# First ordinary tile of three feed-forward blocks in two other PSUM banks, norm factor spread one item earlier, eight weight loads issued behind a barrier

## The reference

```
def swiglu(x, w_gate, w_up, w_down):
    return (jax.nn.silu(x @ w_gate) * (x @ w_up)) @ w_down

for layer in range(2):
    h = h + 0.5 * swiglu(rms_norm(h, norm_ffn[layer, 0]), ...)     # ffn2 (layer 0), ffn4 (layer 1)
    hn = rms_norm(h, norm_mix[layer])
    h = h + (pool_fox_mixer(hn, ...) if layer == 0 else mla_mixer(hn, ...))
    h = h + 0.5 * swiglu(rms_norm(h, norm_ffn[layer, 1]), ...)     # ffn3 (layer 0), ffn5 (layer 1)
```

## Time and profile before

| | before |
| --- | --- |
| three runs, us | 2809.74, 2806.75, 2810.09 (median 2809.74) |
| profiled execution: its own time | 2809.01 us |
| its span, first to last instruction | 2807.1 us |
| PE busy | 2697.0 us (96% of the span) |
| DVE busy | 1757.4 us (63%) |
| ACT busy | 1122.8 us (40%) |
| mean granted TensorE clock | 0.982 |

### The profile page before, as it was taken

How to read it: one execution, slowest core, us unless ns; L and a number is a source line. 1 busy time by engine, 2 the same in 40 slices (tenths; PEclk the granted TensorE clock), 3 DMA queues, 4 the chain that set the end, 5 groups by cost and what they waited for, 6 DMA issues and landing times. The chain is left out here.

```text
span 2807.1 us, 46580 instructions
## 1 busy us (share of the span) xinstructions
PE 2697.0 (96%) x18452; PEld 2263.1 (81%) x18452; DVE 1757.4 (63%) x3031; ACT 1122.8 (40%) x2077; POOL 358.6 (13%) x261
## 2 busy tenths in 40 slices
PE   7989898999999999999999999999999989999998
PEld 5868755778888788888868999989999845889997
DVE  3454668453232643335457888888888656688885
ACT  3232235522211421213265444454444446654444
POOL 2000123421112230212301000010000100100000
PEclk9999989999999999999999999999999999999999
DMA  8250310123332233323303333333332340323331
GB/s 274 62 166 23 103 38 5 61 85 96 96 100 82 83 105 93 102 81 111 88 7 85 99 102 102 95 102 98 91 113 83 75 109 1 90 76 106 98 106 53
DMA packets 346456, 248.75 MB, mean 89 GB/s; under 512 B 28148, under 2 KB 341304, under 8 KB 346240
## 3 DMA queue, kind: packets, MB, share of 16 engines
q1 hardware_dynamic: 346034, 245.71, 29.3%
q10 hardware_dynamic: 206, 0.06, 0.0%
HBM read 241.52 MB, written 2.12 MB: 87 GB/s over the span
## 5 line engine op out<-in xcount | busy, mean ns | idle before, releaser
L2972 ACT CAST dense_wt_hi<-ring 128x512 fp32r<-128x512 f32 x554 | 343.1, 621 | 350.0 <-PE bank L3023 177.5
L2977 DVE TENSOR_TENSOR dense_wt_lo<-ring,dense_wt_hi 128x512 fp32r<-128x512 f32 x554 | 381.6, 691 | 99.8 <-ACT dense_wt_hi L2972 98.9
L3010 PE MATMUL bank<-dense_operand_hi,dense_wt_hi 128*128 128x256 f32 x960 | 272.9, 284 | 7.5 <-DVE h L3500 6.7
L3012 PE MATMUL bank<-dense_operand_hi,dense_wt_lo 128*128 128x256 f32 x960 | 272.3, 284 | 0.0
L3011 PE MATMUL bank<-dense_operand_lo,dense_wt_hi 128*128 128x256 f32 x960 | 272.2, 284 | 0.0
L575 DVE TENSOR_TENSOR dense_wt_lo<-ring,dense_wt_hi 128x2048 fp32r<-128x2048 f32 (+1 forms) x67 | 166.3, 2482 | 155.2 <-ACT dense_wt_hi L560 155.2
L560 ACT CAST dense_wt_hi<-ring 128x2048 fp32r<-128x2048 f32 (+1 forms) x67 | 124.4, 1857 | 306.7 <-PE bank L802 301.1
L3023 PE MATMUL bank<-dense_act_hi,dense_wt_hi 128*128 128x512 f32 x656 | 203.8, 392 | 1.0 <-DVE dense_act_lo L3289 1.0
L3023 PE MATMUL bank<-dense_act_lo,dense_wt_hi 128*128 128x512 f32 x656 | 202.8, 390 | 0.0
L3023 PE MATMUL bank<-dense_act_hi,dense_wt_lo 128*128 128x512 f32 x656 | 202.3, 390 | 0.0
L802 PE MATMUL bank<-feat_lo,dense_wt_hi 128*128 128x512 f32 x640 | 197.1, 389 | 0.0
(11 more groups left out here) (702 smaller groups left out, 5900.7 us busy)
## 6 DMA issues: line engine op xcount, KB each, us to landing
ring<-in_ffn_w_up SPq DMA_DIRECT2D x66, 512.0 KB, 3.8
ring<-in_ffn_w_gate SPq DMA_DIRECT2D x66, 512.0 KB, 5.1
ring<-in_ada_w SPq DMA_DIRECT2D x24, 1024.0 KB, 7.5
ring<-in_ffn_w_down SPq DMA_DIRECT2D x40, 512.0 KB, 4.8
ring<-in_ffn_w_down SPq DMA_DIRECT2D x48, 256.0 KB, 3.8
ring<-in_w_ffn_gate SPq DMA_DIRECT2D x11, 1024.0 KB, 5.4
ring<-in_w_ffn_up SPq DMA_DIRECT2D x11, 1024.0 KB, 5.4
ring<-in_ffn_w_gate SPq DMA_DIRECT2D x11, 1024.0 KB, 5.3
```

Of the source, the lines that this page charges most:

```text
L2972: self.nc.scalar.copy(self.wh[:, i % BLOCKS, :], src).then_inc(self.s_high, 1)
L2977: self.nc.vector.tensor_tensor(self.wl[:, i % BLOCKS, :], self.items[i][1], self.wh[:, i % BLOCKS, :].bitcast(F32), ALU.subtract).then_inc ...
L3010: pe.matmul(out, h[:, w], xh, start=start and k == 0, stop=False, skip_group_check=shared)
L3012: last = pe.matmul(out, l[:, w], xh, start=False, stop=stop and k == 3, skip_group_check=shared)
```

## The change

Tile 0 of each of the three blocks goes to banks 4 and 5; tile 1 stays in 2 and 3. The column sums and the spread factor move from banks 4 and 5 to 6 and 7. P1 and P5 of tile 2 no longer wait for tile 0's product. Items 0 and 1 get a wait for the previous part's additions out of banks 4 and 5. The spread is issued ahead of item 5 instead of item 6. The eight loads at the end of the MLA preparation are issued by SP in the attention stage, behind the barrier.

```
         for b in range(TB):
-            last = pe.matmul(K.bank[4][:, b:b + 1], K.h[:, 0, b * P:(b + 1) * P], K.k("ones")[:, 0:1], start=True, stop=True)
+            last = pe.matmul(K.bank[6][:, b:b + 1], K.h[:, 0, b * P:(b + 1) * P], K.k("ones")[:, 0:1], start=True, stop=True)
...
-            last = pe.matmul(K.bank[5][:, b * P:(b + 1) * P], self.col[:, b:b + 1].broadcast_to([P, P]), K.k("ident"), start=True, stop=True)
+            last = pe.matmul(K.bank[7][:, b * P:(b + 1) * P], self.col[:, b:b + 1].broadcast_to([P, P]), K.k("ident"), start=True, stop=True)
...
-    wide = lambda u, m: K.bank[2 * (u % 2) + m][:, :]
+    wide = lambda u, m: K.bank[(4, 2)[u] + m][:, :]
...
+            if n in (0, 1):
+                pe.wait_ge(prev.done[0], prev.done[1] - 2)
+
...
-            if p in ("P1", "P5") and u < PLAIN + 2:
+            if p in ("P1", "P5") and u == PLAIN + 1:
                 pe.wait_ge(s_act, u - 1)
+            elif u == PLAIN and p in ("P1", "P5"):
+                pass
...
-            if n == 6:
+            if n == 5:
                 now.spread(pe)
...
                         sp.dma_start(B.Q[64:96, 4 * g + j, :], K.h[32 * j:32 * j + 32, g, :]).then_inc(s_moved, 16)
-                K.stream(sp, plan.end("mla_v") + RING)
                 sp.wait_ge(s_moved, 16 * 18)
...
-                        bias=lambda h, i: B.mask[:, 384 - i * P:384 - i * P + (i + 1) * P])
+                        bias=lambda h, i: B.mask[:, 384 - i * P:384 - i * P + (i + 1) * P],
+                    loads=lambda sp: K.stream(sp, K.plan.end("mla_v") + RING))
```

More of the change, by code:

```diff
@@ L3222, in root @@
         act.wait_ge(self.s_sum, 1)
-        K.nc.scalar.activation(self.col[:, :], K.bank[4][:, 0:TB], ACT.Sqrt, bias=K.k("eps")[:, 0:1], scale=1.0 / D).then_inc(self.s_root, 1)
+        K.nc.scalar.activation(self.col[:, :], K.bank[6][:, 0:TB], ACT.Sqrt, bias=K.k("eps")[:, 0:1], scale=1.0 / D).then_inc(self.s_root, 1)
     def inverse(self, dve):
@@ L3238, in factors @@
         act.wait_ge(self.s_spread, 1)
-        self.nc.scalar.copy(K.rs[:, :], K.bank[5][:, :]).then_inc(self.s_rs, 1)
+        self.nc.scalar.copy(K.rs[:, :], K.bank[7][:, :]).then_inc(self.s_rs, 1)
 def out_blocks(K, sec, name, gain):
```

## The result

| | before | after |
| --- | --- | --- |
| runs beside each other, us | 2809.74, 2806.75, 2810.09, 2810.73 | 2796.33, 2793.61, 2790.82, 2794.69 |
| median, us | 2809.91 | 2794.15 |
| profiled execution | 2809.01 | 2796.33 |
| its span, mean granted clock | 2807.1, 0.982 | 2794.5, 0.984 |

The ratio of the runs is 0.9943, 95% interval 0.993 to 0.9956: faster by 15.8 us. The forecast was 2798.6 and its range began at 2794.5, so the time lies 0.35 us outside. The profiled executions differ by 12.7 us.

A forecast was written before the change was run, and what follows sets the result against it. PE was taken as the bound, so only its waits and slow stretches could be gained: blocks 3.1 + barrier 4.8 + clock 2.7 = 10.6 us off 2809.0, stated as 2798.6; 8-in-10 range 2794.5 to 2803.5.

The forecast's parts named there:

- The two steps in DVE's list: Blocks: item 12 still waits for DVE, its wait growing to 2.77 us; gain 1.7 us in ffn5, 0.6 in ffn4.
- The chain of 8.76 us: ffn5: from DVE's scaling of tile 1's gate to item 12's start, 8.76 us, in the same order after the change.
- three groups of waits: PE's waits at item 8 (6.0 us), at the barrier into the MLA attention (5.9) and at item 12 (6.7).
- The spread and not the banks: Blocks: the spread 2.9 us earlier in ffn4 is to free DVE in time; gain booked under tile 0's banks.
- The barrier: Barrier into MLA attention: with SP free, PE starts 0.45 us after ACT's value copy, at 2290.57; 4.8 us gained.
- The clock at the attention's start: MLA attention, first scores to first transposes: full clock after the shorter wait, 2.7 us gained, bounds 0 and 3.2.
- The half clock behind the longer wait: Item 12: all three blocks pay 1.5 us of half clock, new only in ffn3, leaving 0.8 of its 2.28 us.
- its first rival: Blocks: no half clock behind the merged waits, 1.5 us per block spared; two or three spared: chance 0.15.
- Full clock at the attention's start came, so that rival is out: MLA attention starts on the half clock all the same; only the barrier's 4.8 us come there: 2801.3, chance 0.10.
- The loads in flight did not slow it: Rival: loads disturb the attention's first 13.1 us; at 2.5 times as long the time is 2818, chance 0.03.
- The blocks did gain: Rival: blocks gain nothing because DVE sets the pace, and ffn3 pays the half clock too: 2803, chance 0.08.
- the barrier was freed: Rival: the barrier isn't freed because SP waits for something else, such as its last moves landing: 2805.9, chance 0.05.

The follow-up runs named there:

- Banks alone: Changed kernel with the spread back ahead of item 6 and the loads back ahead of the barrier: median 2805.6 us, ratio 1.0 to the kernel before.
- spread alone: Kernel before with only the spread moved ahead of item 5, tile 0 in its old banks: median 2795.4 us, ratio 0.9967.
- loads only: Kernel before with only the eight loads moved behind the barrier: median 2797.2 us, ratio 0.9972.
- the run with the barrier's wait filled: Kernel before plus 34 small identity matmuls on PE while SP issues the eight loads: median 2802.4 us, ratio 0.9982.

## Why the prediction was right or wrong

**The two steps in DVE's list: right.** Item 12 as the point that the blocks' gain is measured at, the wait moved there and grown to 2.77 (2.83 measured), 1.7 us gained in ffn5 (1.97) and 0.6 in ffn4 (0.88), ffn4's wait of 0.8 us for the reciprocal (0.69) all came as worked out. The chain of 8.76 us was 0.22 us shorter after the change, which is most of the small excess in ffn5. (Where the prediction adds up its three groups of waits, the change aims at the first and the second, 6.0 + 5.9 = 11.9 us, and not at the first and the third.)

**The spread and not the banks: said in the text, and shown by runs.** The prediction gave the earlier spread the part of freeing DVE, yet booked the gain under the banks. Banks alone gave 0.7 us at equal clock, spread alone 5.2.

**The barrier: right.** 4.8 us by the end of ACT's copy plus 0.45; the wait fell by 4.96, since PE now starts 0.30 us behind that copy (2287.51 to 2287.81). *The clock at the attention's start* was the term of 2.7 us; it measured 3.1. I had taken fox's 3.79 us from scores to transposes, and MLA, with 18 matmuls there instead of 30, took 3.38.

**The half clock behind the longer wait: right in the trace, mis-sized as a difference.** ffn3 paid 1.49 us behind item 12, as booked (1.5). But its place in the sum was taken from one execution of the kernel before, in which ffn3 had its stretch behind item 8, where it cost 0.6 us (9.10 us against 8.52) and shortened item 12's wait to 1.63 us. In the trace of loads only, ffn3 waits 2.02 + 2.54 us like the other blocks and has its stretch behind item 12. Against that, the merged wait of 2.83 us saves 1.7 us and pays no new stretch, where the prediction had 0.8. Nor did stretches become more frequent with the merged wait: 8 of 9 blocks had one with the old waits, 8 of 12 with the merged ones. That term was some 0.9 us too small on this count.

**The step that failed is that the clock in the rest of the program was held fixed**: the sum puts a difference there at nothing, and the range, "2794.5 to 2803.5, which has the 3.3 us between the runs of before in it too", allows for 3.3 us. The runs of this kernel are not 3.3 us apart but 16, and they follow the mean granted clock. Where the stretches fall differs from run to run all over the program: before 1500 us, where nothing was changed, the ten experiments' and the two main traces lost between 26 and 39 us of clock (one less the granted clock, added up over the microseconds). The prediction allowed for such a draw only inside the blocks, in its first rival, and did not apply it to the comparison as a whole.

In the pair of main traces the gain adds up so: blocks 3.9 us (2.54 - 1.49 + 0.88 + 1.97, forecast 3.1), barrier 4.96 (4.8), attention's start 3.11 (2.7), which makes 12.0 for the change against the 10.6 forecast. The rest of the 12.7 us is 1.42 from the input stage of MLA and -0.74 + 0.02 from the first and the last stretch of the table. Over all runs the change gains 12.2 us, uncertain by 1.9, so the forecast of 10.6 is within that, and the other 3.6 us of the first result are most likely the draw. That the time fell outside the range, by 0.35 us, is most likely luck of the four runs in the main; the term above makes up the rest.

**The rivals.** Full clock at the attention's start came, so that rival is out. The loads in flight did not slow it. From the first scores to ffn5's column sums are 149.10 us with the loads issued in the attention, and 149.05 us in the run with the barrier's wait filled, which issued them ahead of the barrier and had the full clock too. The blocks did gain, and the barrier was freed.

## What to carry to other kernels

Here a wait for a buffer that sat on top of another engine's full queue moved when the buffer was freed, and shortened only when something in that queue moved: look at what the releaser was doing ahead of the release before adding banks. SP's loads held this barrier as an engine's work would, so loads that nobody needs in a stage are worth trying behind it. Where single runs differ by their granted clock, put the time against the clock over many runs before reading a difference of a few tenths of a per cent, and take a stretch of half clock in one trace as a draw, not as a term.

## What the runs showed of the hardware

Eight loads of 512 KB occupied SP for about as long as they took to move. Ahead of the barrier they took 13.09 us, and the trace lists 2.1 us of waits for chunks that PE was still reading; behind it, with every chunk free, they still took 11.9 us (2287.76 to 2299.67), with a median of 1.67 us for one. The rows are of SP's loads before and after (least, median and longest ns, first and last start):

```profile
L213 SPq DMA_DIRECT2D ring<-in_mla_w_out x8: 583/1616/3808, 2281.8 to 2293.0; - x8
```

```profile
L213 SPq DMA_DIRECT2D ring<-in_mla_w_out x8: 373/1670/2541, 2287.8 to 2298.0; - x8
```

512 KB in 1.67 us are 314 GB/s, about what windows of 1 us show as moved from 2290 to 2295 (268 to 334 GB/s), so SP seems to be held by the pace of the transfers; no run tried smaller loads. At item 12, a wait of 0.82 us behind filler matmuls (three blocks) or one of 1.44 us (three blocks) was not followed by the lower clock level; one of 2.8 us was in 10 of 14 blocks, and those of 2.0 and 2.5 us were in some blocks and not in others of one and the same list. The one pair of rows that prices a stretch behind item 12 gives 1.5 us. Over 55 runs of one kernel the time followed the mean granted clock at 1.95 us for each 0.001, and that reduces their standard deviation from 4.2 us to 1.3 us.
